# Attention's bias table held eight times in device memory, one kernel on one core of a Trainium2 chip

## The reference

```python
row_b = (row_idx - r[:, None]) + (WIN_ROWS - 1)
col_b = jnp.clip(ck[None, :] - cq[:, None] + (WIN_COLS - 1), 0, 2 * WIN_COLS - 2)
bias = rpb[:, row_b[:, None, :, None], col_b[None, :, None, :]].astype(jnp.float32)
s_loc = jnp.einsum('brqhd,brkwhd->bhrqkw', q, kg).astype(jnp.float32) * ATTN_SCALE + bias[None]
s_loc = jnp.where(valid_col[:, None, :], s_loc, -jnp.inf)
```

## Time and profile before

| | |
|---|---|
| time, median of three runs (range) | 1320.46 us (1318.17 to 1323.54) |
| the profiled execution: its own time, and its span from first to last instruction | 1320.7 us, 1318.9 us |
| PE busy, share of the span | 1247.3 us, 95% |
| DVE, ACT, POOL busy | 392.1, 332.1, 37.7 us |
| moved by DMA | 535.45 MB, mean 406 GB/s |
| of this POOL's queue q0 | 5.17 MB, 1.1% of the sixteen engines' span |
| chain that ended last | PE 86%, DMA 7%, DVE 4%, ACT 2%, issue 1% |

### The profile page before, as it was taken

The page is one execution under the profiler, slowest core; times in us unless marked ns, Lnnn a source line. Parts: engine busy times, 40 slices in busy tenths (PEclk is TensorE's granted clock), DMA queues, the critical chain, the costliest instruction groups (busy, mean ns, idle before and its releaser), DMA issues.

```text
span 1318.9 us, 17286 instructions
## 1 busy us (share of the span) xinstructions
PE 1247.3 (95%) x6581; PEld 563.0 (43%) x6581; DVE 392.1 (30%) x884; ACT 332.1 (25%) x714; POOL 37.7 (3%) x76
## 2 busy tenths in 40 slices
PE   3879999999899999999999899999999989999996
PEld 0434434343756644443434354443443454434342
DVE  1242213222232324221332324222231452213324
ACT  1141212122221223221212233221221452212122
POOL 2100000000200000000100000000000000000000
PEclk9879999999999999999999999999999999999998
DMA  9999999999999988999999999999999999999994
GB/s 371 420 420 421 421 421 421 421 420 421 398 368 409 394 335 360 422 421 421 420 420 421 421 407 399 422 421 421 420 421 421 415 421 418 422 420 420 422 420 182
DMA packets 87279, 535.45 MB, mean 406 GB/s; under 512 B 11192, under 2 KB 13336, under 8 KB 25760
## 3 DMA queue, kind: packets, MB, share of 16 engines
q1 hardware_dynamic: 82336, 527.47, 97.3%
q0 software_dynamic: 3120, 5.17, 1.1%
q10 hardware_dynamic: 1744, 1.73, 0.4%
HBM read 532.20 MB, written 2.12 MB: 405 GB/s over the span
## 4 chain that ended last, share of the span: by engine, by line
PE 86%; DMA 7%; DVE 4%; ACT 2%; issue 1%; SPq 0%; DVEq 0%; ACTq 0%
PE ps L1939 33%; PE ps L1988 15%; PE ps L1925 5%; PE ps L2000 5%; PE ps L1614 4%; PE ps L1451 4%; PE ps L1576 4%; DMA ring<-in_ada_w_dram 4%; PE ps L1971 3%; PE ps L1623 2%; DMA ring<-in_attn_wqkv_dram 2%; DMA ring<-in_moe_w_down_dram 2%; PE ps L1956 1%; PE ps L1548 1%; ACT hT L707 1%; PE ps L1485 1%
## 5 line engine op out<-in xcount | busy, mean ns | idle before, releaser
L1941 PE MATMUL ps<-ring,xg 128*64 128x512 f32 x968 | 438.0, 597 | 0.0
L1939 PE MATMUL ps<-ring,xg 128*64 128x512 f32 x912 | 412.5, 597 | 2.8 <-DMA ring<-in_moe_w_up_dram 2.8
L1988 PE MATMUL ps<-ring,gb 128*64 128x512 f32 x992 | 225.6, 595 | 0.3 <-DMA ring<-in_moe_w_down_dram 0.3
L1939 PEld LDWEIGHTS ps<-ring,xg 128*64 128x64 f32 x912 | 117.5, 137 | 228.4 <-issue 218.7
L1375 DVE SCALAR_TENSOR_TENSOR gb<-ps,gslot,g2x 128x512 f32<-128x512 f32 x128 | 90.2, 746 | 248.3 <-PE ps L1988 248.3
L1988 PEld LDWEIGHTS ps<-ring,gb 128*64 128x64 f32 x992 | 68.7, 137 | 134.4 <-issue 126.8
L1941 PEld LDWEIGHTS ps<-ring,xg 128*64 128x64 f32 x968 | 124.8, 136 | 0.0
L885 ACT ACTIVATE y_hi<-gb 128x512 fp32r<-128x512 f32 x128 | 77.1, 627 | 169.0 <-PE ps L2000 109.1
L1451 PE MATMUL ps<-ring,cact 128*32 128x512 f32 x768 | 93.0, 618 | 12.9 <-DMA ring<-in_ada_w_dram 7.2
L872 ACT ACTIVATE gu<-ps 128x512 f32<-128x512 f32 x64 | 38.3, 598 | 246.5 <-PE ps L1941 246.5
L1384 DVE TENSOR_TENSOR y_lo<-gb,y_hi 128x512 fp32r<-128x512 f32 x128 | 83.6, 688 | 12.5 <-ACT y_hi L885 11.9
(11 more groups left out here) (221 smaller groups left out, 1127.2 us busy)
## 6 DMA issues: line engine op xcount, KB each, us to landing
ring<-in_moe_w_down_dram SPq DMA_DIRECT2D x124, 1024.0 KB, 17.4
ring<-in_moe_w_up_dram SPq DMA_DIRECT2D x121, 1024.0 KB, 16.8
ring<-in_moe_w_gate_dram SPq DMA_DIRECT2D x114, 1024.0 KB, 17.3
ring<-in_ada_w_dram SPq DMA_DIRECT2D x96, 1024.0 KB, 17.7
ring<-in_attn_wqkv_dram SPq DMA_DIRECT2D x12, 1024.0 KB, 21.6
spare<-in_moe_w_down_dram SPq DMA_DIRECT2D x4, 1024.0 KB, 23.7
xh<-in_moe_w_up_dram SPq DMA_DIRECT2D x4, 1024.0 KB, 21.0
hT<-in_moe_w_gate_dram SPq DMA_DIRECT2D x4, 1024.0 KB, 22.5
```

Of the source, the lines that this page charges most:

```text
L1939: mg = pe.matmul(ps[0:SLOTS, B_GU, :], xg[:, b, e, :], wg[:, i * F:(i + 1) * F], start=(b == 0), stop=(b == DB - 1))
L1941: mu = pe.matmul(ps[SLOTS:P, B_GU, :], xg[:, b, e, :], wu[:, i * F:(i + 1) * F], start=(b == 0), stop=(b == DB - 1))
L1988: mm = pe.matmul(ps[r * SLOTS:(r + 1) * SLOTS, DOWN_BANKS[e % 2], :], acts[:, e % ACTS, j, :], w[:, i * D + r * HALF:i * D + (r + 1) * HAL ...
```

## The change

The device memory tensor becomes eight tables of four rows each (the fourth row is not written), so that one table takes 32 KB. The first is written as before. POOL then copies it within device memory: table 0 to table 1, tables 0 and 1 to 2 and 3, tables 0 to 3 to 4 to 7, waiting for each copy before the next. The four reads take partition q's window from table q modulo 8. The semaphore that counts these transfers reaches 9 times 16 instead of 6 times 16, and POOL's wait ahead of the reads stands now ahead of the loads of `ck` and `cv`.

```diff
+COPIES = 8
...
-        bias_dram = nc.dram_tensor("bias_rows", [3, P, HEADS], F32, kind="Internal").ap()
+        bias_dram = nc.dram_tensor("bias_rows", [COPIES, 4, P, HEADS], F32, kind="Internal").ap()
...
-            pool.dma_start(bias_dram.rearrange("d p h -> p d h"), rback[:, :, :]).then_inc(s_bias, 16)
+            pool.dma_start(bias_dram[0, 0:3].rearrange("d p h -> p d h"), rback[:, :, :]).then_inc(s_bias, 16)
             for t in range(2, 4):
                 ada_bias(t)
+            copied = 1
+            while copied < COPIES:
+                pool.wait_ge(s_bias, 32 + 16 * (copied.bit_length() - 1))
+                pool.dma_start(bias_dram[copied:2 * copied, 0:3], bias_dram[0:copied, 0:3]).then_inc(s_bias, 16)
+                copied *= 2
+            pool.wait_ge(s_bias, 16 * 5)
...
-            pool.wait_ge(s_bias, 32)
             for r in range(2):
                 for kr in range(2):
                     src = bass.AP(tensor=bias_dram.tensor, offset=((kr - r + 1) * P + 1) * HEADS,
-                                  ap=[[HEADS, GRID_W], [1, GRID_W * HEADS]])
+                                  ap=[[COPIES * HEADS, GRID_W // COPIES], [(4 * P + 1) * HEADS, COPIES], [1, GRID_W * HEADS]])
...
-                v.wait_ge(s_bias, 16 * 6)
+                v.wait_ge(s_bias, 16 * 9)
```

## The result

The changed kernel takes 1327.63 us, the median of ten runs from 1323.91 to 1329.00, and the kernel before 1321.76 us, the median of ten from 1318.17 to 1324.20. The medians lie 5.9 us apart. The ratio is 1.0039, with a 95% interval from 1.0030 to 1.0049: 0.39% or 5.2 us slower (4.0 to 6.5 us). The forecast was 1320.0 us with a range up to 1325.5: the sign is wrong, and the time lies outside. The profiled execution of the changed kernel, 1323.91 us with a span of 1322.0, is the shortest of its ten, so its rows show less of the loss at the very end than the medians do.

What follows compares the result with a forecast made beforehand. Transfers were taken to bound layer 0 and the experts, PE layer 1's attention. Against the profiled execution 1320.7 - 1.4 + 0.9 = 1320.2 us, so 1320.0 us for the median; range 1316.0 to 1325.5 us.

Steps and rivals of the forecast that it cites:

- the four reads: Layer 1 attention: spreading reads over eight tables brings the values' load forward and removes PE's 1.41 us stop.
- the copies: Layer 0: copies within device memory hold a DMA engine and delay the first query weights, 0.9 us.
- The first rival: Table reads: eight tables read as slowly as one, or the writing side limits; 1321.4 us, chance 0.28.
- the second rival: Table reads: eight engines carry each read, lengthening PE's wait by 2.5 to 7.0 us; 1323.9 to 1328.4 us, chance 0.09.
- the copies' upper bound: Layer 0 copies: 2.9 us if both hit the same engines, +2.0 about the value taken.
- The waits on POOL: Layer 0: each copy waits for the one before, hidden by POOL's idle time until 348.71 us; cost 0.
- The path: Chain of waits: transfers to 338.95 us, PE through attention and most of layer 1's experts, then a transfer issued at 733.23.
- the rival that all lost DMA time counts: From 379 us on: transfers are the limit, so the lost 4.5 us reach the end; 1316.9 us, chance 0.06.

Runs made afterwards that it cites:

- e4: Kernel before, its four reads taking 256 KB each of the cached keys and values instead of the table: 1320.81 us, ratio 0.9996.
- e3: Changed kernel with four tables instead of eight, read as sixteen rows of four pieces: 1321.67 us, ratio 1.0004 to the kernel before.
- e7: Kernel before, one table, with two reads over all 128 partitions instead of four over 64; biases not the reference's: 1319.06 us, ratio 0.9975.
- e10: As e7, but each read told as 16 groups of 8 neighbouring partitions: 1322.01 us, ratio 0.9997 to the kernel before.
- e2: Kernel before, no copies, one table, reads told as eight rows of eight pieces: 1325.21 us, ratio 1.0029.
- e11: Kernel before, reads of partitions 0 to 63 on POOL's queue and 64 to 127 on ACT's, cache loads divided likewise: 1319.11 us, ratio 0.9976.
- e6: As e2, but reads told as four rows of sixteen pieces: 1327.12 us, ratio 1.0039 to the kernel before.
- e1: Changed kernel with its copies, but all four reads take table 0 in the form of before: 1326.18 us, ratio 1.0038 to the kernel before.
- e5: As e1, with each copy cut into sixteen rows of 1.5 KB per table: 1322.34 us, ratio 1.0003 to the kernel before.
- e8: Changed kernel with its copies cut into sixteen rows, reads of eight tables kept: 1325.82 us, ratio 1.0026 to the kernel before.
- e9: Against the kernel before: four copies build 16 blocks of biases per read, two reads fill 128 partitions; reference's biases: 1321.16 us, ratio 0.9999.

## Why the prediction was wrong, step by step

Three steps failed: the four reads, put at a gain of 1.41 us, made the values' load 1.7 us late by their new form; the copies, put at 0.9 us, made it 2.2 us late; and the clock behind a stop of PE was put at nothing.

**The four reads: here it failed, and first in its premise.** "If reading one 8 KB stretch by all engines at once is what slowed the 13 us, and eight tables spread it": e4 reads elsewhere and is as slow, e3 reads four tables and gains nothing in time. The reason given for the choice, that `ck` and `cv` ran at 418 GB/s through the same queue, compared loads into 128 partitions with reads into 64, so it spoke as much for the writing side. The first rival had it right that the writing side is short, and the argument against it was wrong: 182 GB/s into one half was said to be under a limit that 209 shows to be possible. But 209 was reached by transfers that fill all 128 partitions; e7 and e10 fill the same partitions with the same bytes and differ by 95 GB/s, so a rate per half says nothing. That it counts which partitions are filled at the same moment is the likely reading; no run shows it directly. From the first to the last 4 KB packet of the reads, before, e7, e10, e2 and after:

```profile
360.00:372.00 12.00, 12.00 (x72) 9.18 (x74) 0.69 (x1) 3.50 (x5) 0.00 (x0) 1.00 1.03 270
```

```profile
358.50:365.90 7.40, 7.40 (x36) 6.51 (x35) 0.00 (x0) 0.60 (x1) 0.00 (x0) 1.00 1.02 417
```

```profile
358.50:369.30 10.80, 10.80 (x64) 8.81 (x66) 0.69 (x1) 2.48 (x5) 0.00 (x0) 1.00 1.03 287
```

```profile
359.10:375.50 16.40, 16.40 (x112) 10.55 (x115) 0.69 (x1) 3.50 (x5) 0.00 (x0) 1.00 1.03 262
```

```profile
359.20:375.60 16.40, 15.84 (x107) 9.97 (x105) 0.69 (x1) 3.50 (x5) 0.00 (x0) 1.00 1.04 261
```

Two numbers make the loss, the rate and how long it lasts. At 418 GB/s the bytes of before's 12.0 us would have taken 7.8 us, so 4.2 us are lost; e7 loses nothing. The changed kernel's rate is nearly before's, but it lasts 16.4 us: 6.2 us lost, an estimate from these rows.

The Trainium skill names a mechanism (SBUF — State Buffer, section Door 1: The DMA port swizzle; DMA: Bandwidth & Descriptors, section The descriptor swizzle): in a plain transfer to 128 partitions each engine writes a port of its own, while 64 partitions reach eight of the sixteen ports. The rates agree in their order, 403 GB/s for the first (e7) and 272 for the second. By its map 16 groups of 8 neighbours, walked in step, meet eight ports at a time as well, and e10's 308 agrees. e11, whose reads fill both halves at once, moves only 292 GB/s meanwhile, so the map alone doesn't settle it; no trace here shows a port.

**The reads in their new form: the second rival's mechanism, which got a chance of 0.09.** It put 2.5 to 7.0 us on the stop of PE at 377.84; the form alone makes qkv 4 1.7 us late (e2), and fours, which it didn't consider, are worse again (e6). The range left it out in part: 1323.9 with the copies' upper bound of 2.0 more is 1325.9, over the end of 1325.5. I had argued that two confined reads cover all engines and the extra vanishes. It doesn't: all sixteen engines are late. The Trainium skill (DMA: Bandwidth & Descriptors, section Why a DMA increments its semaphore by 16 and not by 1) says that the engines of a transfer are the largest number up to 16 that divides both slowest dimensions; e3, e2 and e6, with 16, 8 and 4, agree in their order. I used that rule against the rival and should have counted it for it.

**The copies: the right size at the place that I watched, and too small at the one that decides.** The term was 0.9 us, one piece of 24 KB on one engine, and the first query weights arrive 0.6 us late (339.5 against 338.9), in e1 0.9. That was taken for the whole price. But at the values' load, in the slow stretch, e1's last engine is 2.2 us late, inside the upper bound of 2.9 that I had worked out for both copies on the same engines. e5 confirms that the copies' shape does it: the same bytes in sixteen pieces leave 0.6 us. A lag of single engines is slow to go in a stream that never stops: measured by the spread between a load's first and last engine, e1 is 2.0 us over before at 90 to 120 us, 1.5 at 200 to 300 and 1.0 at 300 to 335. PE pays the lag where it waits, 0.9 us at qkv 0 and the rest, up to 2.2, at qkv 4; why it is larger there again isn't shown.

**What was missing: the clock behind a stop.** In eight traces PE stood for over 2 us ahead of the values (e1, e2, e3, e4, e8, e9, e10 and after; 2.23 to 4.24 us), and in each they took 8.6 to 8.8 us, at a granted clock from 380 to 400 us of 0.91 to 0.94. In e6, after 3.69 us, they took 9.82 at 0.83. After 1.41 (before) or 1.57 us (e5), or no stop (e7, e11), they took 7.06 to 7.11 at 1.00. No term or bound of mine held these 1.5 to 2.7 us.

But they are not a price of the change alone, since the same work can go either way. Ahead of the first query products eleven of the thirteen traces have the same stop of 1.97 to 2.00 us. In five (before, e1, e5, e6, e11) the granted clock from 339 to 344 us is then 0.66, and in before the products take 29.55 us; in six (after, e3, e4, e7, e9, e10) it stays at 1.00. The clock's fall in before's trace is hidden, as PE would only have waited longer for the values. Without it PE arrives earlier, stands longer for the same load, and the clock falls there. So it is in e4 (its lines are one lower), which does the same as before until its reads at 348 us, and whose load of the values lands at 378.9 us, no later than before's:

```profile
339.09 27.87 PE ps L1613 x128
...
376.29 2.73 issue
379.02 8.80 PE ps L1622 x16
```

e4's values end at 387.82 us, 1.5 us after those in before's trace, and its median is no worse. So after, which had no fall at 339 us either, is 5.1 us late against before's trace at the end of the values and 3.7 against e4's. How often either case occurs in the runs without a profile isn't on record.

The sum as measured, at the end of the values: landing 3.4 us (copies 2.2 and form 1.7 apart) and, against before's trace, clock 1.7 make 5.1, where the forecast had -1.4 + 0.9. That is within the interval of the ratio (4.0 to 6.5 us); 3.7 lies a little under it. The losses of e1 and e2, 4.9 and 3.9 us by their medians, make 2.9 more than the changed kernel's 5.9: one fall of the clock counted twice would be 1.7 of it, the rest isn't shown.

**What held.** The waits on POOL cost nothing: three copies landed within 6.7 us each, long before POOL's next work at 348 us. The path was read rightly: the place is PE's wait for qkv 4, and the DMA engines' idle time takes what doesn't hold PE up. Their share from 440 to 520 us went from 0.89 to 0.86, so in that stretch they are not the limit, which speaks against the rival that all lost DMA time counts:

```profile
440.00:520.00 80.00, 79.12 (x432) 38.49 (x432) 22.34 (x49) 19.80 (x56) 5.22 (x10) 1.00 0.86 336
```

The times alone don't exclude that rival: e7's load of the values lands 4.1 us earlier than e4's, and its ratio means a gain of 2.0 to 4.5 us.

The gain of 1.41 us for a stop that goes was the right size in one pair of traces only: e11's values end 1.4 us earlier than before's, with a fall of the clock at 339 us in both. Without that fall in either, e7's end 4.5 us earlier than e4's, since the fall at the values goes with the stop. The ratios of e7 and e11 lie between, at 1.9 to 4.5 us, so 1.41 was too small there.

## What to carry to other kernels

Before a transfer is made faster by moving its source, vary the source alone in one run and the destination's partitions alone in another: here another source changed the time by nothing that could be measured (e4), and the way in which the partitions were filled changed it (e7 and e10). Look at how the transfer's dimensions are told, too: the same bytes by eights cost 3.9 us (e2). In a stream that keeps all DMA engines full, cut an extra transfer into at least sixteen pieces: the copies cost 4.9 us with two and four pieces of 24 KB (e1) and nothing measurable with sixteen rows (e5). Price a stop of PE by its length and by the clock after it, and compare two traces only after looking at where the clock fell in each.

## What the runs showed of the hardware that was not expected

- Reads that filled 64 partitions slowed the transfers beside them: 270 GB/s in all while they moved, against 418 just before. Reads that filled 128 in one run didn't (417, e7), and the same 128 told as 16 groups of 8 did (287, e10). The weights' own packets of 8 KB took 491, 314 and 468 ns meanwhile.
- Reads of both halves from two queues at once were hardly faster in all (292 GB/s, e11), but were over after 8.2 us instead of 12.0.
- By eights and by fours a read of 64 pieces came with more packets of 4 bytes, and the four reads were in motion for 16.4 and 18.1 us instead of 12.0 (e2, e6).
- Copies within device memory of 48 and 96 KB, in pieces of 24 KB, left engines behind in a full stream: the spread between the first and the last engine of a load, averaged over the loads that landed from 90 to 120 us, was 4.2 us in e1 against 2.2 before and 2.5 with the copies in 16 pieces; at 380 us, 300 us after the copies, the last engine was still 2.2 us late.
- Ahead of the values every stop of 2.2 us and more was followed by 1.5 to 2.7 us lost at a lower granted clock, and those of 1.4 and 1.6 us by none. Elsewhere the length doesn't tell: after the same stop of 2.0 us at 337 us the clock fell in five traces and stayed in six.
